# Norms summed partly on TensorE, a shorter inverse root, constant matmuls in four norms, and a memory region placed 128 bytes later

## What is computed

```
def rms_norm_2(x, gain=None):
    xf = x.astype(jnp.float32)
    y = xf * lax.rsqrt(jnp.mean(xf * xf, axis=-1, keepdims=True) + EPS)
```

```
    x = x + g_m * (y @ w_out)
    h = rms_norm_2(x) * (1 + sc_f) + sh_f
    gate, up = jnp.split(h @ w_ffn_in, 2, axis=-1)
    x = x + g_f * ((jax.nn.silu(gate) * up) @ w_ffn_out)
```

## Time and profile before

| | us |
|---|---|
| median of 3 runs (range) | 1924.19 (1923.92 to 1924.31) |
| the profiled execution, its own time | 1918.18 |
| its span (first to last instruction) | 1916.3 |
| PE busy | 1789.7 (93% of the span) |
| DVE busy | 980.6 |
| POOL busy | 792.4 |
| ACT busy | 722.7 |
| mean granted TensorE clock | 0.969 of full |

### The profile page before, as it was taken

How to read it: one execution, slowest core, us unless ns; L and a number is a source line. 1 busy time by engine, 2 the same in 40 slices (tenths; PEclk the granted TensorE clock), 3 DMA queues, 4 the chain that set the end, 5 groups by cost and what they waited for, 6 DMA issues and landing times. The chain is left out here.

```text
span 1916.3 us, 23439 instructions
## 1 busy us (share of the span) xinstructions
PE 1789.7 (93%) x8351; PEld 1446.4 (75%) x8353; DVE 980.6 (51%) x1729; ACT 722.7 (38%) x1238; POOL 792.4 (41%) x368
## 2 busy tenths in 40 slices
PE   4988989999899999899999999899999899999997
PEld 4865767877778776778888887778776778888885
DVE  7989698756559876243323210559876131101112
ACT  4332365652266454232212222266454232222221
POOL 3345233417354510544445535254510544444442
PEclk9988998999899999999999999899999999999998
DMA  5433132307233210345555422233310222223211
GB/s 212 143 110 121 45 100 78 100 1 270 70 110 99 91 53 12 110 140 189 176 176 197 165 88 88 67 110 99 99 45 12 88 78 98 88 96 102 99 55 44
DMA packets 56057, 197.66 MB, mean 103 GB/s; under 512 B 6929, under 2 KB 7953, under 8 KB 55698
## 3 DMA queue, kind: packets, MB, share of 16 engines
q1 hardware_dynamic: 55954, 196.26, 30.3%
HBM read 194.14 MB, written 2.10 MB: 102 GB/s over the span
## 5 line engine op out<-in xcount | busy, mean ns | idle before, releaser
L453 POOL TENSOR_TENSOR WL<-RAW,WH 128x1024 fp32r<-128x1024 f32 x260 | 662.6, 2554 | 928.2 <-ACT WH L534 712.2
L1578 PE MATMUL bank<-HH,WH 128*128 128x512 f32 x1120 | 440.3, 393 | 11.8 <-POOL WL L453 8.5
L1580 PE MATMUL bank<-HH,WL 128*128 128x512 f32 x1120 | 438.7, 392 | 0.0
L1579 PE MATMUL bank<-HL,WH 128*128 128x512 f32 x1120 | 438.6, 392 | 0.0
L534 ACT ACTIVATE WH<-RAW 128x1024 fp32r<-128x1024 f32 x260 | 271.3, 1051 | 267.4 <-PE bank L1580 241.1
L1578 PEld LDWEIGHTS bank<-HH,WH 128*128 128x128 f32 x1120 | 212.0, 189 | 58.4 <-issue 7.5
L1580 PEld LDWEIGHTS bank<-HH,WL 128*128 128x128 f32 x1120 | 211.9, 189 | 44.7
L1579 PEld LDWEIGHTS bank<-HL,WH 128*128 128x128 f32 x1120 | 212.1, 189 | 44.1
L1514 DVE TENSOR_TENSOR HF<-SILU,bank 128x512 f32<-128x512 f32 x44 | 30.3, 688 | 338.8 <-PE bank L1580 333.3
L1578 PE MATMUL bank<-HDH,WH 128*128 128x512 f32 x352 | 139.1, 395 | 0.0
L1580 PE MATMUL bank<-HDH,WL 128*128 128x512 f32 x352 | 139.0, 395 | 0.0
(11 more groups left out here) (320 smaller groups left out, 2932.0 us busy)
## 6 DMA issues: line engine op xcount, KB each, us to landing
RAW<-in_stream SPq DMA_DIRECT2D x364, 512.0 KB, 3.3
X<-in_xt SPq DMA_DIRECT2D x2, 1024.0 KB, 6.2
out_t<-YA SPq DMA_DIRECT2D x8, 256.0 KB, 2.0
ACC<-in_pos SPq DMA_DIRECT2D x1, 256.0 KB
gains<-in_gains SPq DMA_DIRECT2D x1, 224.0 KB
CS<-in_cs SPq DMA_DIRECT2D x1, 128.0 KB
cw<-in_cw SPq DMA_DIRECT2D x1, 128.0 KB
par<-in_par SPq DMA_DIRECT2D x1, 115.0 KB
```

The source lines that it names most:

```text
L453: nc.gpsimd.tensor_tensor(lo(k)[:], raw(k)[:], hi(k)[:].bitcast(F32), ALU.subtract).then_inc(sem["passed"], mark("passed", *k))
L1578: nc.tensor.matmul(out, A[0], B[0], start=first, stop=False)
L1579: nc.tensor.matmul(out, A[0], B[1], start=False, stop=False)
L1580: return nc.tensor.matmul(out, A[1], B[0], start=False, stop=last)
```

## The change

It has four parts.

1. `W0` is 128 bytes larger: the small tensors end at 7,776, which was rounded up to 7,808 (30.5 x 256) bytes past a kilobyte, and is now 7,936 (31 x 256).
2. POOL (DVE in n1) no longer adds the square of tile 7. PE multiplies the total of tiles 0 to 6 with ones as soon as it is there, then the square of tile 7, into the same PSUM column. The factor 1/1024 moves into the square.
3. `rsqrt` has 9 operations in place of 11: the first guess in one, then one step of third order and one of second.
4. In m0, f0, m1 and f1 PE multiplies constants (`identb` with `keep`, bf16, 128x512) into banks that nobody reads: 7 times behind "ss", 6 times behind "rb".

```diff
-        W0 = (cur[0] + 63) // 64 * 64
+        W0 = (cur[0] + 63) // 64 * 64 + 128
...
             def add_squares(tag, sq, total, key_of=None):
-                for k in range(1, KD):
+                for k in range(1, KD - 1):
                     if key_of:
                         pass_through(key_of(k))
...
+                if key_of:
+                    pass_through(key_of(KD - 1))
...
-                nc.scalar.activation(sq[:, k % 2, :], X[:, k, :], ACT.Square).then_inc(
+                nc.scalar.activation(sq[:, k % 2, :], X[:, k, :], ACT.Square, scale=float(D) ** -0.5).then_inc(
...
             def rsqrt(y, v, t):
+                p = lt[0:y.shape[0], 4:6].rearrange("p a l k -> p (a l k)")[:, 0:y.shape[1]]
-                V.tensor_scalar(y.bitcast(I32), v.bitcast(I32), 1, None, ALU.arith_shift_right).then_inc(
+                V.tensor_scalar(y.bitcast(I32), v.bitcast(I32), -0.5, float(0x5F3759DF), ALU.mult, ALU.add).then_inc(
...
-                for _ in range(3):
...
+                V.tensor_tensor(t, y, y, ALU.mult).then_inc(step, 1)
+                V.tensor_tensor(t, t, v, ALU.mult).then_inc(step, 1)
+                V.tensor_scalar(p, t, 0.375, -1.25, ALU.mult, ALU.add).then_inc(step, 1)
+                V.tensor_tensor(p, p, t, ALU.mult).then_inc(step, 1)
+                V.scalar_tensor_tensor(out=y, in0=p, scalar=1.875, in1=y, op0=ALU.add, op1=ALU.mult).then_inc(step, 1)
+                V.tensor_tensor(t, y, y, ALU.mult).then_inc(step, 1)
+                V.scalar_tensor_tensor(out=t, in0=t, scalar=-0.5, in1=v, op0=ALU.mult, op1=ALU.mult).then_inc(step, 1)
+                V.scalar_tensor_tensor(out=y, in0=t, scalar=1.5, in1=y, op0=ALU.add, op1=ALU.mult).then_inc(step, 1)
...
-                V.tensor_scalar(stat[:, 0, :], b[:, 0:NT], 1.0 / D, EPS, ALU.mult, ALU.add).then_inc(
+                V.tensor_scalar(stat[:, 0, :], b[:, 0:NT], EPS, None, ALU.add).then_inc(
...
-            for k in range(1, KD):
+            for k in range(1, KD - 1):
                 dve.wait_ge(sem["square"], value("square", "n1", k))
...
-            def norm(tag, total):
+            def norm(tag, total, newest):
...
                 b = claim("ss", tag)
+                pe.wait_ge(sem[adder], value(adder, tag, KD - 2))
                 for tt in range(NT):
+                    nc.tensor.matmul(b[:, tt:tt + 1], total[:, tt * P:(tt + 1) * P], ones[:, 0:1],
+                                     start=(tt == 0), stop=False)
+                pe.wait_ge(sem["square"], value("square", tag, KD - 1))
+                for tt in range(NT):
+                    last = nc.tensor.matmul(b[:, tt:tt + 1], newest[:, tt * P:(tt + 1) * P], ones[:, 0:1],
+                                            start=False, stop=(tt == NT - 1))
                 full(last, "ss", tag)
+                warm(tag, 0, 7)
                 b = claim("rb", tag)
                 pe.wait_ge(step, value("rstd", tag))
...
                 full(last, "rb", tag)
+                warm(tag, 1, 6)
+
+            def warm(tag, i, n):
+                if tag not in ("n1", "fin"):
+                    b = claim("warm", tag, i)
+                    for _ in range(n):
+                        nc.tensor.matmul(b[:], identb[:], keep[:], start=True, stop=True)
```

More of the change, by code:

```diff
@@ L910, in rsqrt @@
             def rsqrt(y, v, t):
-                V.tensor_scalar(y.bitcast(I32), v.bitcast(I32), 1, None, ALU.arith_shift_right).then_inc(
+                p = lt[0:y.shape[0], 4:6].rearrange("p a l k -> p (a l k)")[:, 0:y.shape[1]]
+                V.tensor_scalar(y.bitcast(I32), v.bitcast(I32), -0.5, float(0x5F3759DF), ALU.mult, ALU.add).then_inc(
                     step, 1)
                 dve.wait_ge(step, own())
-                V.tensor_scalar(y.bitcast(I32), y.bitcast(I32), -1.0, float(0x5F3759DF), ALU.mult, ALU.add).then_inc(
-                    step, 1)
+                V.tensor_tensor(t, y, y, ALU.mult).then_inc(step, 1)
                 dve.wait_ge(step, own())
-                for _ in range(3):
[L919 to L926, removed]
+                V.tensor_tensor(t, t, v, ALU.mult).then_inc(step, 1)
+                dve.wait_ge(step, own())
+                V.tensor_scalar(p, t, 0.375, -1.25, ALU.mult, ALU.add).then_inc(step, 1)
+                dve.wait_ge(step, own())
+                V.tensor_tensor(p, p, t, ALU.mult).then_inc(step, 1)
+                dve.wait_ge(step, own())
+                V.scalar_tensor_tensor(out=y, in0=p, scalar=1.875, in1=y, op0=ALU.add, op1=ALU.mult).then_inc(step, 1)
+                dve.wait_ge(step, own())
+                V.tensor_tensor(t, y, y, ALU.mult).then_inc(step, 1)
+                dve.wait_ge(step, own())
+                V.scalar_tensor_tensor(out=t, in0=t, scalar=-0.5, in1=v, op0=ALU.mult, op1=ALU.mult).then_inc(step, 1)
+                dve.wait_ge(step, own())
+                V.scalar_tensor_tensor(out=y, in0=t, scalar=1.5, in1=y, op0=ALU.add, op1=ALU.mult).then_inc(step, 1)
+                dve.wait_ge(step, own())
             def norm(tag, tmp, gain, shift):
@@ L1717, in hidden @@
                                       start=False, stop=True), "hid", kv)
-            norm("n1", SQS)
+            norm("n1", SQS, RELU[:, (KD - 1) % 2, :])
             project(0)
@@ L1848, in _ @@
                 tag = f"m{L}"
-                norm(tag, SQ2)
+                norm(tag, SQ2, SQT[:, (KD - 1) % 2, :])
                 h = h_pair(tag)
@@ L1987, in _ @@
                             mods(fo_slot(L, half, n))
-            norm("fin", SQ2)
+            norm("fin", SQ2, SQT[:, (KD - 1) % 2, :])
     return note
```

8 lines of the change are left out of this document (3 added, 5 removed).

## The result

The changed kernel takes 1895.13 us (median of 4 runs, 1893.11 to 1895.43) against 1924.06 before (4 runs, 1922.42 to 1924.31): ratio 0.9849, 95% interval 0.9832 to 0.9866, 28.9 us less. The prediction was 1895.

A forecast was written before the change was run, and what follows sets the result against it. PE, busy 1789.7 of 1916.3 us, was taken as the bound, losing time to norm waits, half clock and dearer products. Norms and heads 22.6 less 2.5, 20.1, plus region 8.8 gave 28.9: 1924.19 to 1895 us, range 1888 to 1908.

The forecast's parts named there:

- n1: Norm n1: eight more PE instructions on the path, one DVE add off it; root ends 0.2 us earlier.
- m0: Norm m0, clock kept: last add 1.2, shorter root 0.4, full-clock "rb" 0.95, products behind 1.0; 3.5 us.
- f0: Norm f0, clock kept: last add 1.33, shorter root 0.4, full-clock "rb" 0.95, products behind 2.7; 5.4 us.
- m1: Norm m1, clock kept: add 3.1, full-clock "ss" 0.8, root 0.4, "rb" 0.95, products behind 1.0; 6.3 us.
- f1: Norm f1, clock kept: add 1.33, "ss" 0.3, root 0.4, "rb" 0.95, products behind 1.7; 4.7 us.
- head roots: Head norms: two operations fewer per call; two calls ahead of PE's wait for SCORE save 0.8 us, others counted nothing.
- fin: Norm fin: last add on PE 1.33 and shorter root 0.4; 1.7 us.
- region: Products with an operand moving from behind W0: 1440 at 6.1 ns less each, 8.8 us, if start address causes the excess.
- Rival A: Products behind W0: the region does nothing, excess comes from place or other readers; 1904 us, chance 0.25.
- C: Products behind W0 get dearer from the shift, kernel slower by over 0.2%; 1933 us at 20 ns more, chance 0.02.
- B: Norms: clock falls before the constants everywhere, gain 10.1 us; 1905 with the region's gain, 1914 without; chance 0.10.
- D: Whole kernel: mix of B without the region, head roots hidden; within 0.2% of before, 1922 us, chance 0.03.

The follow-up runs named there:

- region + 64: Changed kernel with W0 64 bytes later than in the kernel before, in place of 128: 1904.50 us, ratio 0.9902 to the kernel before.

## Why the prediction was right

The forecast of 28.9 us equals the measured 28.9, but that is closer than the method can be: the interval of the ratio reaches 3.3 us to either side, terms were off by up to 1.5 us, and the falls of the clock differ from profile to profile. The mechanism held in the main in all four parts; the last digit is luck.

Each term against the two traces (from landmark to landmark: the starts of the last product ahead of a norm, of the first behind it, and of the last one of the stage behind that):

| term | predicted | measured | how |
|---|---|---|---|
| n1 | 0.2 | 0.3 | first token product at 28.24, was 28.50 |
| head roots | 0.8 | 0.6 | up to the product behind `SCORE` |
| m0 | 3.5 | 3.1 | 2.05 to the tokens, 1.04 in them |
| f0 | 5.4 | 4.8 | 2.65 to the dense pair, 2.12 behind |
| m1 | 6.3 | 4.8 | 4.83 to the tokens, nothing in them |
| f1 | 4.7 | 4.1 | 2.99 and 1.10 |
| fin | 1.7 | 1.4 | to the end |
| region | 8.8 | 8.7 | `HDH` 6.75, `YH` 1.92 |

Norms and heads make 19.1 where 20.1 had been forecast (22.6 with the clock held everywhere, less 2.5), and with the region 27.8 against 28.9. The 2.5 stood for a clock that falls in two of four norms. Through the norms it fell in m0 alone here, and most of the 3.5 us between 22.6 and 19.1 were lost elsewhere, as told below: the deduction had about the right size for other reasons than its own. Between the two profiles 4.6 us were lost in attention, as above, and 2.0 won between the m and f norms, in stages that the change doesn't touch: 27.8 - 4.6 + 2.0 = 25.2, the 25.0 between the spans.

**The last add.** Right: in f0 the square ends at 807.41 and the newest square's products run from 807.47 to 808.52, with ACT as their releaser: 1.1 us behind the square, as said. The run with POOL's add back puts its price at 13.9 us where the terms give 8.3 to 9.1; the traces put the rest at falls of the clock, which the prediction had booked with the constants and which one profile can't assign. In m0 "ss" ended 1.6 us earlier relative to the last product, where 1.2 had been forecast.

**The root.** 0.4 us in f0, f1 and fin, as said, but not in every norm. In m1 the first of the ten operations took 0.59 us in place of 0.16 and ended within 0.02 us of POOL's subtraction beside it. With the add gone, the root of m1 now comes while POOL passes a weight slot, as it did in n1 in the earlier trace rows, and nothing of the 0.4 is left (2.55 us from "ss" to "rb", 2.52 before). In m0 the root was done at 487.65, but the constants, at half clock, kept PE until 488.04.

**The constants.** Right in kind, and in size as far as the runs can tell: (0.9888 - 0.9849) and (0.9888 - 0.9844) of 1924 are 7.5 and 8.5 us by the run without them, each uncertain by nearly 5 us; the prediction had 0.95 four times, 2.7, 1.7 and 1.0 twice, less 2.5, which is 7.7. The pair behind f0 ends 1.1 us behind the last `HL` and not 0.5, the 0.6 that f0 fell short. "rb" was at full clock in f0, m1 and f1 and not in m0, one norm better than "two of four"; in the other profiles with this code it was often worse. The Trainium skill, page "TensorE: Matmul & The Clock Gate", Part 1, has the unit that watches activity run freely, and not reset when a kernel starts, from which the prediction took that the same code could hold the clock in one norm and not in the next. The traces agree with that much: the same code of f0 held the clock in two profiles (7.98 us) and not in five (8.8 to 8.9 us). That a free-running unit is the reason, no run here shows.

**m1, the term that was most off.** 6.3 us forecast, 4.8 measured: 0.4 are the root's, as above, and 1.0 had been taken for the tokens behind the norm, as for m0. The clock held through the norm and then fell at 1196.0, 2.1 us into the tokens. PE had stood idle for 1.26 us ahead of the first product and 0.52 ahead of the fourth, since six constants end 1.3 us too early there. That idle time alone does not make the clock fall: m0's tokens have the same 1.26 and 0.52 us and stayed at full, and so did m1's tokens with six constants in the runs without the region, with the base moved, with region + 64, with the weights moved and with the old root. With eleven constants the idle time is 0.18 us, and neither m0's nor m1's tokens have a stretch at half clock.

**The region.** Right in size, wrong in one half of its reason. The prediction gave 1440 products at 6.1 ns if "the excess comes from the start address"; it is the start address relative to the weights', as the runs with the base and with the weights moved show. Rival A (the region does nothing) is out, and with it C; B (no clock held) and D fall with the full-clock "rb" in three norms. The page "SBUF — State Buffer", "Who interferes with whom", of the Trainium skill, which spoke for it, lists two read ports of PE, one for the moving operand and one for the weights, and calls them independent. The 5.7 to 6.6 ns that hang on the offset between the two operands show a coupling that the table doesn't have, and the measurement decides; whether it lies in the ports, no run shows.

**The sum against the median.** The gain was worked out from a profiled execution that was 6 us quicker than the median and subtracted from the median. That was reasonable, since the terms were taken in stages where the two kernels could be compared piece by piece; a difference of whole spans would have given 1899.

## What to carry to other kernels

In these runs fp32r products of 128x512 cost the least when the moving operand and the weights start at the same offset modulo 256 bytes: compare the time of like products in unbroken stretches, by operand, and move whichever tensor is cheaper to move. Where TensorE waits a few us for a chain of small operations, count the time until the last wide product, not the idle time alone, and fill it with products that end just before the data come: with too few the clock may still fall, and each one too many costs 0.2 to 0.4 us. Don't judge from one profile whether the clock holds: the same code held it in two profiles here and not in five. And when a norm starts earlier, look at what its small operations now run beside: in m1, POOL's subtraction took back the 0.4 us of the shorter root. Work out gains stage by stage, for the stage that the change leaves alone can differ by 5 us between two executions.

## What the runs showed of the hardware

- An fp32r product of 128x512 takes 226.7 ns when the moving operand and the weights lie alike modulo 256 bytes, and 232.4 to 233.3 when they are 64 or 128 bytes off, at full granted clock, with no idle time, and whichever of the two was moved.
- PE counts as busy for 3.67 of 3.70 us of products with one column at m0 (482.0 to 485.7), and the granted clock behind them was 0.54. With more constants ahead in the kernel the same products at m0 were not followed by a fall. In the tokens with nearly the same idle time (PE busy for 2.87 and 2.82 of 3.40 us) the clock stayed at 1.00 behind m0 and fell behind m1.
- A DVE operation on 128x4 int32 values took 0.16 to 0.17 us alone and 0.59 us beside POOL's subtraction of 128x1024 in m1.
- A stretch at half clock behind a wait cost 2.7 us behind `SCORE` (46.3 - 43.6) and 1.7 at the last product with V (4.06 - 2.39), where the wait itself can't be shortened. Filling such waits brought 10.7 us beyond the change, from 1892.6 to 1881.9.
